# The pair of experts outside the weight ring eleventh in order instead of seventeenth, and the shared expert's down products beside the early projection

## The reference

```python
scores = sigmoid(x @ w_router)                       # top 4 of 8 groups, then top 8 experts
def expert_step(acc, ew):
    wg, wu, wd, gcol = ew                            # 1024x256, 1024x256, 256x1024
    h = silu(xt @ wg) * (xt @ wu)
    return acc + gcol[:, None] * (h @ wd), None
acc, _ = scan(expert_step, zeros, (w_eg, w_eu, w_ed, gates.T))
f = acc + (silu(xt @ w_sg) * (xt @ w_su)) @ w_sd     # the shared expert
x = layer_norm(ALPHA * x + f)
x = x + sigmoid(x @ w_ple_gate) * (p[i] @ w_ple_proj)
```

## Time and profile before

| | us |
| --- | --- |
| median of three runs | 1626.64 (1623.5 to 1627.1) |
| profiled execution, its own time | 1624.6 |
| its span, first to last instruction | 1622.8 |
| TensorE busy | 1566.7 (97% of the span) |
| VectorE busy | 537.4 (33%) |
| ScalarE busy | 339.4 (21%) |
| TensorE idle until expert weights had landed | 6.4, in 6 places |

### The profile page before, as it was taken

One profiled execution on the slowest core, in us unless ns is written; L12 is line 12 of the kernel. 1 busy time (PEld: TensorE's weight loads), 2 busy tenths in 40 slices (PEclk: granted clock), 3 DMA queues, 4 the chain that ended last, 5 costly groups with the idle time before them and its releaser, 6 DMA issues.

```text
span 1622.8 us, 22336 instructions
## 1 busy us (share of the span) xinstructions
PE 1566.7 (97%) x8226; PEld 788.6 (49%) x8226; DVE 537.4 (33%) x1324; ACT 339.4 (21%) x686; POOL 150.6 (9%) x242
## 2 busy tenths in 40 slices
PE   7998899999999999999999999979999999999998
PEld 5774544344444443466565654554443444444434
DVE  2156522222222222451434334462222122222226
ACT  2211212121212211221222221022121122122122
POOL 0331100000000000000111111020000000000000
PEclk9989999999999999999999999989999999999999
DMA  9633899999989999963567586579999999999980
GB/s 301 259 116 143 349 402 420 420 421 419 419 359 420 420 420 418 385 241 119 175 231 250 184 277 241 201 299 382 420 420 420 420 418 367 420 420 420 420 348 30
DMA packets 121611, 536.17 MB, mean 330 GB/s; under 512 B 17880, under 2 KB 29400, under 8 KB 73791
## 3 DMA queue, kind: packets, MB, share of 16 engines
q1 hardware_dynamic: 98311, 470.35, 72.7%
q0 software_dynamic: 21360, 61.64, 10.4%
q10 hardware_dynamic: 1872, 3.22, 0.6%
HBM read 526.15 MB, written 23.87 MB: 339 GB/s over the span
## 4 chain that ended last, share of the span: by engine, by line
PE 87%; DMA 6%; DVE 4%; issue 1%; ACT 1%; SPq 1%; POOL 0%; ACTq 0%; DVEq 0%
PE ps L1360 24%; PE ps L1387 12%; PE ps L1175 11%; PE ps L1145 11%; PE ps L1300 6%; DMA weights<-in_w_exp_up 5%; PE ps L1353 4%; PE ps L1296 2%; PE ps L1371 2%; PE ps L1380 2%; PE ps L1054 1%; PE ps L1551 1%; PE ps L1317 1%; PE ps L1032 1%; PE ps L1045 1%
## 5 line engine op out<-in xcount | busy, mean ns | idle before, releaser
L1360 PE MATMUL ps<-weights,x_feat 128*64 128x512 f32 x1856 | 408.8, 593 | 8.8 <-DMA weights<-in_w_exp_up 6.4
L1360 PEld LDWEIGHTS ps<-weights,x_feat 128*64 128x64 f32 x1856 | 134.3, 137 | 273.8 <-issue 273.5
L1387 PE MATMUL ps<-weights,arena 128*64 128x512 f32 x992 | 226.5, 598 | 0.9 <-ACT arena L1578 0.9
L1145 PE MATMUL ps<-x_feat,weights 128*128 128x288 f32 x800 | 201.9, 410 | 1.1 <-ACT x_feat L1578 1.1
L1145 PEld LDWEIGHTS ps<-x_feat,weights 128*128 128x128 f32 x800 | 153.7, 194 | 43.5 <-issue 3.8
L2221 DVE CAST split<-state 128x1024 fp32r<-128x1024 f32 (+1 forms) x66 | 44.7, 678 | 325.0 <-ACT state L1578 325.0
L2218 DVE SCALAR_TENSOR_TENSOR arena<-arena,ps 128x256 f32<-128x256 f32 x64 | 30.8, 481 | 352.1 <-ACT arena L1807 352.1
L2605 POOL DMA_INDIRECT arena<-x_rows,arena x64 | 63.6, 994 | 880.3 <-DVE arena L2211 826.3
L1578 ACT ACTIVATE state<-ps 128x512 f32<-128x512 f32 x132 | 78.9, 597 | 287.8 <-PE ps L1387 261.0
L1387 PEld LDWEIGHTS ps<-weights,arena 128*64 128x64 f32 x992 | 65.7, 136 | 132.2 <-issue 130.9
L1807 ACT ACTIVATE arena<-ps 128x256 f32<-128x256 f32 x64 | 24.6, 384 | 432.3 <-PE ps L1360 401.7
(11 more groups left out here) (308 smaller groups left out, 1332.0 us busy)
## 6 DMA issues: line engine op xcount, KB each, us to landing
weights<-in_w_exp_gate SPq DMA_DIRECT2D x124, 1024.0 KB, 13.4
weights<-in_w_exp_up SPq DMA_DIRECT2D x124, 1024.0 KB, 16.4
weights<-in_w_exp_down SPq DMA_DIRECT2D x124, 1024.0 KB, 15.0
weights<-in_w_in_c SPq DMA_DIRECT2D x24, 1024.0 KB, 8.8
arena<-in_state_ret POOLq DMA_DIRECT2D x20, 512.0 KB, 5.5
out_ret_sample<-arena POOLq DMA_DIRECT2D x20, 512.0 KB, 6.6
weights<-in_w_in_a SPq DMA_DIRECT2D x8, 1024.0 KB, 10.7
weights<-in_w_ple_gate SPq DMA_DIRECT2D x8, 1024.0 KB, 18.2
```

The lines of the kernel that those rows point to most:

```text
L1145: last = pe.matmul(ps[:, 0:T], lhs(c), XT[:, c, :], start=(c == 0), stop=(c == n - 1))
L1360: last = pe.matmul(ps[64 * s:64 * s + 64, :], XGT[u][:, c, 64 * s:64 * s + 64], rhs, start=(c == 0), stop=(c == KC - 1))
L1387: last = pe.matmul(ps[64 * s:64 * s + 64, :], HT[u][:, c, 64 * s:64 * s + 64], wd[s][:, c, 512 * n:512 * n + 512], start=(c == 0), stop=(c ...
```

## The change

The home pair is moved from place 16 to place 10. The written-out iterations move with it: they were 6, 7 and 8 and are now 4 and 5, and the loop behind them is 6 to 11 where it was 9 to 11. `shared_down` is no longer between places 11 and 12 but before `early_projection`, between places 23 and 24. All uses of `HOME` follow: SyncE's first loop of refills now ends three iterations earlier, and the load of `w_ple_proj` now follows `gate_up` of place 10. Nothing is added and nothing is left out.

```diff
-HOME = 16
+HOME = 10
@@
                 two_pairs(0)
-                with pe.Fori(1, HOME // 2 - 2) as it:
+                with pe.Fori(1, HOME // 2 - 1) as it:
                     two_pairs(it)
-                shared_down()
-                for it in range(HOME // 2 - 2, HOME // 2 + 1):
+                for it in range(HOME // 2 - 1, HOME // 2 + 1):
                     two_pairs(it)
                 with pe.Fori(HOME // 2 + 1, PROJECT_AT) as it:
                     two_pairs(it, True)
+                shared_down()
                 early_projection()
                 with pe.Fori(PROJECT_AT, PAIRS // 2 - 1) as it:
                     two_pairs(it, True, True)
```

## The result

The changed kernel takes 1637.7 us, median of four runs (1636.76 to 1639.51); the kernel before takes 1625.9 (four runs, 1623.5 to 1627.1). The ratio is 1.0070, 95% interval [1.0057, 1.0083]. That is 11.8 us more, where the forecast's sum was 1.3 us more and 1631.5 the upper end of its range.

A forecast was written before the change was run, and what follows sets the result against it. TensorE was taken to bound the kernel except where the ring of weights runs dry. Terms -9.8 + 11.4 - 0.3 = +1.3 us gave 1625.9 on the profiled execution; 1627 was taken, range 1622 to 1631.5 with 8 in 10.

The forecast's parts named there:

- the small edits: Minor terms: a place behind other work happens once less a layer, -0.3 us in both; loop against written-out code, 0.
- The clock: Rival: several waits over 1 us in a row at the pairs could lower TensorE's clock; chance 2 in 100.
- The term of the stalls up to place 23: Places 19 or 20 to 23: new waits for ring weights, 1.3 us each, 5.7 us a layer, 11.4 in both.
- the landing of place 13's weights: Place 13: gate and up weights land at about 368 us, due at 376.1, so slack is 7.8 us.
- the cap of an empty queue: Place 13: weights issued up to 355.5 us land 12.8 us later, at 368.3.
- the time in line behind `w_ple_proj`: Place 13: previous pair's landing plus one pair plus that load, 349.7 + 15.9 + 2.5 = 368.1 us.
- stalls above 7 us a layer (p over 16.0): Sign of being wrong: waits for ring weights larger than forecast, with over 16.0 us between landings of two ring pairs.
- the waits at 10 and 11: First ring stalls in each layer, forecast to go: -2.93 and -2.40, together -5.3 us.
- the standstill at place 16: DMA idle with a full ring at the old home pair, 5.9 us between 446 and 487 us; forecast to go.
- the lump: `shared_down` and the early projection together before place 24: gives the ring 12.7 us back, ending the last stalls, -4.5 us.
- The second rival: Slower: ring runs dry earlier and deeper at places 18 to 23, +3.3 us at p = 16.0, +5.3 at 16.1; chance 0.22.
- the first rival: Faster: mean rate of bytes sets 15.61 us a ring pair, sum -4.5 us, thus 1622.5; chance 0.14.

The follow-up runs named there:

- the second megabyte: Changed kernel with `w_ple_proj` loaded a second time beside the first load, 2 x 512 KB more a layer: 1643.31 us, ratio 1.0099 to the kernel before.

## Why the prediction was wrong

- **The step that failed** is in the small edits: "One written-out iteration less and one more turn of a loop: the ten places 14 to 23 are partly one, partly the other, and are even, so 0." I asked only whether a turn of a loop runs as fast as written-out code. It does. But the iteration taken out, some 320 instructions, also shifts all code behind it, and behind the jump over the untaken branch TensorE now needs code that has not arrived. It cost 8.4 us in the trace. Shown: putting the length back removes it (1637.7 to 1631.07), taking the length from the other kernel makes it (1638.9), and code that never runs makes it (1635.97). That the late thing is a block of TensorE's code follows from this, from the q8 packet in the gap and from the count of such packets (49, 47, 51). Where in the code a block begins was not looked for, so that which length is safe cannot be said from these runs.
- The Trainium skill, Runtime: NRT & Kernel Launch, section "Instruction fetch mechanics", states this mechanism: code comes in blocks of 16 KiB by DMA, ahead of use only in sequence, and "Branching breaks sequential prefetch". The packets of 16.4 KB and the never-run experiment agree. The wait was 3.4 to 5.8 us beside a full DMA queue here, and 1.9 us beside an almost idle one.
- **The clock** was a rival with 2 in 100, at the ring's waits of 1.6 us, and they never lowered it. The granted clock was 1.00 from 440 to 540 us. The fetch gap did lower it: 0.50 after 5.35 us.
- **The term of the stalls up to place 23** was mis-sized, its mechanism right. Forecast: 5.7 us a layer, 11.4 in both; measured: 530.60 - 318.60 - 203.98 = 8.0 and 1444.23 - 1233.51 - 203.98 = 6.7, 14.8 in both. Two inputs of its sum were off: the landing of place 13's weights, and p, the time between the last landings of two ring pairs. In layer 0 the refill of place 13, with its last issue at 356.42, landed 14.1 us later and not 12.8:

```profile
356.42 0.69 SPq L744 DMA_DIRECT2D weights<-in_w_exp_up  x1
...
507.52 0.38 SPq L744 DMA_DIRECT2D weights<-in_w_exp_up  x1
```

```profile
DMA to landing us min/median/max: 6.8/10.4/14.1
...
DMA to landing us min/median/max: 12.6/17.6/22.8
```

  And p was (507.52 + 22.8 - 356.42 - 14.1) / 10 = 15.98 where I took 15.9: together 1.3 + 0.8 = 2.1 of the 2.3 us. In layer 1 the landing took 13.4 and p was 15.95. I took the cap of an empty queue and the time in line behind `w_ple_proj` as alternatives, of which the later counts (368.3 and 368.1). That they were so close that they partly added fits the 14.1 us, but is a reading and not shown. The prediction's sign of being wrong, "stalls above 7 us a layer (p over 16.0)", came in layer 0 without its reason: p stayed under 16.0.
- **Right:** the waits at 10 and 11 went; none stands at 24 to 31; the waits of the long stretch came at 18 to 23 (0.4 to 1.6 us each, at six places in layer 0 and at 19 to 23 in layer 1); the standstill at place 16 went and a dip followed the lump. The lump costs 7.07 and 1.00 for the shared products and 4.63 for the projection, as before.
- **The second rival** (slower, p from 16.0) had the right sign and place, and at 15.98 it was nearly met. Without the fetch the order costs +5.8 us in the runs (ratio 1.0036 [1.0022, 1.0050]) and +4.2 in the changed kernel's trace, about where that rival was priced (+3.3 to +5.3). By its own sum p of 15.98 and 15.95 gives +2.6, and the later landings at place 13 add 1.3 and 0.6, together 4.5. The rest of the 11.8 is the fetch, which no rival named. The rate of bytes (15.61) as the first rival took it is refuted: over the ten pairs of layer 0 the queue moved 63.99 MB in 159.8 us, 15.71 us a pair by bytes, while the landings came every 15.98.

## What to carry to other kernels

A change of how many iterations are written out, or of any code ahead of a jump, is a change of where later code stands. Look up each taken jump behind it for a wait put down to "issue" and for an instruction packet beside it, and vary the length with code that never runs before believing that an order is slower.

With two resources that are nearly even and a small buffer between them, work that gives slack back is worth its time only where the buffer has room: spread it, and put it where the buffer first runs dry. A load moved from a standstill of the queue into a busy stretch costs what the queue has no spare time for: all 2.5 us of the second megabyte here, at most 1.3 of the first.

## What the runs showed of the hardware that was not expected

- TensorE waited 3.4, 4.5, 4.5, 5.4 and 5.8 us for code behind a jump while weights filled the DMA queues, and 1.9 us when they were nearly empty. The packet of code was at work some 2 to 4 us before TensorE went on.
- After such a wait beside full queues eight matmuls took 6.5 to 6.6 us for 3.45 (5.8 after one of the 4.5 us waits), with the granted clock at 0.50 to 0.52. After the 1.9 us it stayed at 1.00. Waits of up to 1.6 us every 16 us left it at 1.00.
- The last landing of a ring pair came every 15.9 to 16.0 us over ten pairs, though the bytes by themselves would take 15.61 to 15.71. Which of the 16 engines is late was not looked for.
